# Selection mask of the sparse attention: from a TensorE matmul to a GpSimd add ahead of the logits

## The chip, the cores and the metric

The kernel runs on one core of a Trainium2 chip. The metric is the device time of one execution in microseconds (us), median of three runs. Engines are called by their names in the profile where rows are quoted: PE is TensorE (PEld its weight loads), DVE is VectorE, ACT is ScalarE, POOL is GpSimd, SP issues the DMAs.

## What is computed

Two transformer blocks one after the other on one sequence of 512 tokens of width 1024, in float32. The first has a convolution and retention mixer and an MLP. The second has two kinds of attention with 8 heads of 64 each, a gated merge of the two, and an MLP. The change concerns the second kind of attention, in which every query sees only the keys that an indexer selected:

```python
_, sel = lax.top_k(iscore, topk)               # topk = 128
...
logits = jnp.einsum('bqhd,bqkhd->bhqk', qb, kg) * scale
bias = rel_bias[t5_bucket(dist)]
logits = logits + jnp.transpose(bias, (0, 3, 1, 2))
logits = jnp.where(valid[:, None], logits, -jnp.inf)
p = jax.nn.softmax(logits, axis=-1)
```

The first kind ("forgetting attention") is dense and causal, with a per-key term in place of the bias.

## The kernel before

The kernel is written engine by engine, and each engine runs its instructions in the order written; the order between engines is set by semaphores. There is no planner: what an engine does next is what stands next in its program.

**Precise products.** A float32 product is made of three matmuls on rounded parts: high by high, high by low, low by high. For every 128-column block of weights, SP loads 512 KB into one of four slots of `raw`, ScalarE casts it to `w_hi` (`cast`, L988) and GpSimd makes `w_lo = raw - w_hi` (`lo`, L486). These subtractions are nearly all that GpSimd does. TensorE's `unit` (L526) uses both; it waits for `lo_ready`.

**The attention.** Heads go in pairs: pairs 0 to 3 are the dense attention, pairs 4 to 7 the selected one (`NQ = 4`). A pair has 8 tiles, n = 0 to 7: query block i = n // 2 (128 queries, (i + 1) * 128 keys) of head n % 2. So the tiles of a pair have 128, 128, 256, 256, 384, 384, 512 and 512 keys. "Tile 5.4" below is tile 4 of pair 5. Its way through the engines:

1. `s_step` on TensorE: query times keys into one of two PSUM banks (bank SA for even n, the next for odd n), as two matmuls (L809, L810) and a third that adds the mask through an identity matrix: in pairs 4 to 7 the selection's mask `sel` (L813, bf16, all keys of the tile), in pairs 0 to 3 the causal mask on the last 128 keys (L815). `sel` holds 0 for a selected key and -3e38 for any other. The step waits until the logits of the tile two before it, which used the same bank, are done (`att_logit`).
2. `logits` on VectorE (L1890): adds the table `tab2` (bias by position) to the PSUM bank, scales, writes to the tile's buffer `prob(n)` in SBUF and takes the row's extreme `mneg`. There are four such buffers, so it waits until the transposes of the tile four before are done (`att_t`, `LOOK = 4`).
3. `exps` on ScalarE (L1278), in place, with the row sums.
4. `weights` on VectorE for two tiles at once: a reciprocal (L1896) and two multiplications of `prob` in place (L1899).
5. `t_step` on TensorE: transposes into PSUM (L823); copies out by VectorE (`turned_even`, L1905) and ScalarE (`turned_odd`, `turned_last`); then `pv`, probabilities times values (L836).

**The order of a step.** TensorE's loop goes over p (pair) and n: some steps begin with a `pv`; then come `t_step` of tile p.n, `s_step` of the tile four later, and a piece of a projection: two of the eight k of a `unit`, six matmuls. "Step 4.7" below is this step for p = 4, n = 7. The projections make the queries (slot 0) and keys (slot 1) of pair p + 2, and at the end the first gates of the merge.

VectorE's order (`att`), by n: at even n `weights` of the next two tiles, then `turned_even` (n < 6), then the logits of the tile four later. Besides: at n = 2 `y_lows` (L1909) after the logits, at n = 3 `k_lows` ahead of them (L1925, L1927: low parts of the next pair's keys, for which `s_step` of the next pair's tile 0 waits), at n = 7 `q_lows`, in pairs 0 to 3 rounds of the indexer's selection at n = 1, 4, 5, 6, and in pairs 5 to 7 at n = 2, 4, 5 a piece of the first block's final norm (`final_norm`, L1804, two SBUF inputs).

ScalarE's order, by n of the step: exp of tile n + 4 throughout; `y_evac` and `k_hi` after n = 1; the cast for slot 1 after n = 3; `turned_last` and `q_hi` (two parts) around n = 6; the cast for slot 0 after n = 7.

GpSimd's order in the attention is only `lo` for slot 0 and slot 1 in turn, each as soon as its cast is done. SP loads the weights of a pair, then its table; the table of pair g waits for the logits of pair g - 2, and a slot's load waits for `lo_ready` of that slot.

Of the kernel before, what the change touches and what calls it, by code (L numbers as in the profile page):

```python
# [27 lines left out]
ALU = mybir.AluOpType  # L28
ACT = mybir.ActivationFunctionType

P = 128
T = 512
# [4 lines left out]
NQ = QW // P  # L37
# [17 lines left out]
LOOK = 4  # L55
# [113 lines left out]
def build(nc, tab, x, norm1_g, w_in, conv_w, conv_norm_g, ret_norm_g, w_out, norm2_g, w_up, w_down,  # L169
# [14 lines left out]
    st_att = Stage(st_val, 2 * NQ, 2)  # L184
    st_bra = Stage(st_att, KC, 3, [1, 1, 2, 1])
    bra_order = [(0, 0), (1, 0), (0, 1), (1, 1), (2, 0), (0, 2)]
# [11 lines left out]
    with ctx:  # L198
# [5 lines left out]
        def sem(name):  # L204
            if name not in sems:
                sems[name] = ctx.enter_context(nc.semaphore(name))
            return sems[name]
# [16 lines left out]
        identb, causalb = sb("identb", [P, P], BF16), sb("causalb", [P, P], BF16)  # L224
# [25 lines left out]
        start = ExitStack()  # L250
# [28 lines left out]
        q_up, q_dn = sb("q_up", [P, 4, T], F32R, where=merge), sb("q_dn", [P, 4, T], F32R, where=merge)  # L279
# [5 lines left out]
        k_both = sb("k_both", [P, 4, T], F32R, where=two)  # L285
        tab2 = sb("tab2", [P, 4, T], where=two)
        sel = sb("sel", [P, NT, T], BF16, where=two)
# [25 lines left out]
        def prob(n):  # L313

            return (prob_evens, prob_odds)[n // 2 % 2][:, n % 2, 0:(n // 2 + 1) * P]
# [160 lines left out]
        @block.gpsimd  # L476
        def _(pool):
            for s in range(1, SLOTS):
                pool.sem_inc(lo_ready[s], 1)
            pool.memset(ones[:], 1.0).then_inc(sem("const"), 1)  # L480
            pool.memset(epsc[:], EPS).then_inc(sem("const"), 1)

            def lo(st, s, i):

                pool.wait_ge(hi_ready[s], st.turn(s, i) + 1)
                pool.tensor_tensor(w_lo[:, s, :], raw[:, s, :], w_hi[:, s, :], ALU.subtract  # L486
                                   ).then_inc(lo_ready[s], 1)

            for half in range(2):
                c = slice(half * NQ * P, (half + 1) * NQ * P)  # L490
                pool.wait_ge(hi_ready[0], half + 1)
                pool.tensor_tensor(w_lo[:, 0, c], raw[:, 0, c], w_hi[:, 0, c], ALU.subtract).then_inc(lo_ready[0], 1)
            for s in range(1, SLOTS):
                lo(st_ret, s, 0)
            with pool.Fori(1, NQ) as i:
                for s in range(SLOTS):
                    lo(st_ret, s, i)
            for st in (st_conv, st_out, st_mlp, st_idx, st_val, st_att, st_bra, st_out2, st_mlp2):
                if st is st_bra:
                    for s, m in bra_order:  # L500
                        lo(st_bra, s, m)
                elif st.n == 1:
                    for s in range(st.k):
                        lo(st, s, 0)
                else:
                    with pool.Fori(0, st.n) as i:
                        for s in range(st.k):
                            lo(st, s, i)
# [3 lines left out]
        def _(pe):  # L512
# [287 lines left out]
            def s_step(p, n):  # L800
                i, hh = n // 2, n % 2
                if n == 0:
                    pe.wait_ge(sem("q_ready"), 2 * p + 3)
                    pe.wait_ge(sem("k_ready"), 2 * p + 2)
                wait(pe, sem("att_logit"), 8 * p + n - 1)
                keys = (i + 1) * P
                bank, at = SA + hh, 2 * (p % 2) + hh
                q = slice(i * P, (i + 1) * P)
                pe.matmul(ps[:, bank, 0:keys], q_up[:, at, q], k_both[:, at, 0:keys], start=True, stop=False)  # L809
                pe.matmul(ps[:, bank, 0:keys], q_dn[:, at, q], k_both[:, at, 0:keys], start=False, stop=False)  # L810
                if p >= NQ:
                    pe.wait_ge(sem("sel_ready"), i + 1)
                    last = pe.matmul(ps[:, bank, 0:keys], identb[:], sel[:, i, 0:keys], start=False, stop=True)  # L813
                else:
                    last = pe.matmul(ps[:, bank, keys - P:keys], identb[:], causalb[:], start=False, stop=True)  # L815
                last.then_inc(sem("att_s"), 1)

# [614 lines left out]
        def _(dve):  # L1432
# [446 lines left out]
            def logits(p, n):  # L1879
                keys = (n // 2 + 1) * P  # L1880
                if n == 0:
                    dve.wait_ge(sem("tab_in"), 16 * (p + 1))
                dve.wait_ge(sem("att_s"), 8 * p + n + 1)
                wait(dve, sem("att_t"), 8 * p + n + 1 - LOOK)
                if p < NQ:
                    tab = tab2[:, 2 * (p % 2) + n % 2, 0:keys]
                else:
                    tab = tab2[:, 2 * (p % 2) + n % 2, T - keys:T]

                dve.tensor_tensor_reduce(prob(n), ps[:, SA + n % 2, 0:keys],  # L1890
                                         tab, -(HD ** -0.5), -MASKED, ALU.add, ALU.min,
                                         mneg[:, n:n + 1]).then_inc(sem("att_logit"), 1)
# [141 lines left out]
```

## Time and profile before

| | |
|---|---|
| median of 3 runs (lowest, highest) | 1399.9 us (1398.48, 1400.33) |
| the profiled execution: its time, its span | 1399.89 us, 1398.1 us |
| busy share of the span: PE, DVE, ACT, POOL | 98%, 58%, 37%, 41% |
| the attention of pairs 4 to 7, from the first mask to the last | 780.4 to 859.8 us from the span's start |
| mask matmuls in it (L813) | 32 |

A share of busy time is an average over the whole span; what holds the work up at one place is read from the rows of that place. The end of a matmul in the timeline is modelled, and matmuls overlap, so the cost of one is read from the distances between starts. The profiled execution is within 0.01 us of the median; 1.8 us of it lie outside its span.

### The profile page before, as it was taken

How to read it: one execution, taken by the hardware profiler on the slowest of the kernel's cores; microseconds unless marked ns; L12 is line 12 of the kernel's file. 1: busy time of each engine (PE TensorE's matmuls, PEld its weight loads, DVE VectorE, ACT ScalarE, POOL GpSimd, SP SyncE). 2: the span in 40 equal slices, each digit the busy share in tenths (PEclk: the TensorE clock that was granted, in tenths of full speed). 3: DMA queues.
4: the chain of work that ended last, by engine and by line, in shares of the span. 5: the costliest groups of instructions: out<-in, count | busy, mean ns of one | idle time of the engine just before them, and what ended most of it. 6: DMA issues, size and time to landing. Idle time of an engine off the chain costs nothing.

```text
span 1398.1 us, 18553 instructions
## 1 busy us (share of the span) xinstructions
PE 1369.5 (98%) x6374; PEld 1103.4 (79%) x6374; DVE 808.5 (58%) x1062; ACT 517.7 (37%) x783; POOL 569.4 (41%) x230
## 2 busy tenths in 40 slices
PE   7999999999999999999999999999989999999997
PEld 6777778888888888887777777888868888888886
DVE  4555568584766747886988865343346334252353
ACT  4332224331322314235366664322344223142243
POOL 3433335353562635424322223444425536356341
PEclk9999999999999999989999999999999999999999
DMA  7653234365573754703223232332423323233221
GB/s 205 143 93 95 61 106 156 98 176 157 145 223 108 207 158 131 194 31 109 73 76 91 56 95 77 98 98 81 122 61 113 108 80 113 75 105 109 85 77 60
DMA packets 238993, 155.58 MB, mean 111 GB/s; under 512 B 7860, under 2 KB 229424, under 8 KB 238808
## 3 DMA queue, kind: packets, MB, share of 16 engines
q1 hardware_dynamic: 238472, 153.56, 39.3%
q10 hardware_dynamic: 464, 1.27, 0.3%
q8 instruction: 35, 0.57, 0.2%
q14 instruction: 22, 0.18, 0.0%
HBM read 150.08 MB, written 4.73 MB: 111 GB/s over the span
## 4 chain that ended last, share of the span: by engine, by line
PE 50%; DVE 2%; ACT 1%; issue 0%; POOL 0%; DVEq 0%; ACTq 0%
PE ps L526 40%; PE ps L918 3%; PE ps L836 2%; PE ps L823 2%; PE ps L859 2%; PE ps L809 1%; PE ps L810 1%; DVE work L1871 1%; DVE work L1868 0%; PE ps L813 0%; DVE work L1853 0%; DVE top L1851 0%; POOL w_lo L486 0%; DVE otok L2010 0%; PE ps L815 0%
## 5 line engine op out<-in xcount | busy, mean ns | idle before, releaser
L486 POOL TENSOR_TENSOR w_lo<-raw,w_hi 128x1024 fp32r<-128x1024 f32 x222 | 566.0, 2559 | 796.7 <-ACT w_hi L988 792.1
L526 PE MATMUL ps<-u_hi,w_hi 128*128 128x512 f32 x1016 | 410.5, 404 | 9.9 <-DVE u_lo L1481 3.8
L526 PE MATMUL ps<-u_hi,w_lo 128*128 128x512 f32 x1016 | 398.0, 392 | 0.0
L526 PE MATMUL ps<-u_lo,w_hi 128*128 128x512 f32 x1016 | 397.6, 391 | 0.0
L988 ACT ACTIVATE w_hi<-raw 128x1024 fp32r<-128x1024 f32 x221 | 231.3, 1053 | 233.5 <-PE ps L526 111.6
L526 PEld LDWEIGHTS ps<-u_hi,w_hi 128*128 128x128 f32 x1016 | 192.9, 190 | 52.7 <-issue 8.1
L526 PE MATMUL ps<-y_hi,w_hi 128*128 128x512 f32 x576 | 226.6, 393 | 0.1
L526 PE MATMUL ps<-y_hi,w_lo 128*128 128x512 f32 x576 | 224.2, 389 | 0.0
L526 PE MATMUL ps<-y_lo,w_hi 128*128 128x512 f32 x576 | 224.2, 389 | 0.0
L526 PEld LDWEIGHTS ps<-u_hi,w_lo 128*128 128x128 f32 x1016 | 191.7, 189 | 41.1
L526 PEld LDWEIGHTS ps<-u_lo,w_hi 128*128 128x128 f32 x1016 | 192.3, 189 | 39.0 <-issue 1.9
L1728 DVE TENSOR_TENSOR nt<-nsq 128x512 f32<-128x512 f32 x64 | 82.9, 1296 | 138.1 <-ACT nsq L1184 134.9
L526 PEld LDWEIGHTS ps<-y_hi,w_lo 128*128 128x128 f32 x576 | 108.1, 188 | 22.9
L1750 DVE TENSOR_TENSOR nt<-ps,nrs 128x512 f32<-128x512 f32 x64 | 44.2, 690 | 141.6 <-PE ps L526 138.0
L526 PEld LDWEIGHTS ps<-y_hi,w_hi 128*128 128x128 f32 x576 | 108.2, 188 | 22.4 <-POOL w_lo L486 0.5
L526 PEld LDWEIGHTS ps<-y_lo,w_hi 128*128 128x128 f32 x576 | 108.2, 188 | 21.9 <-issue 0.2
L1184 ACT ACTIVATE nsq<-ps 128x512 f32<-128x512 f32 x64 | 38.0, 594 | 218.5 <-PE ps L526 218.3
L1733 DVE TENSOR_TENSOR y_lo<-nt,y_hi 128x512 f32 x64 | 93.1, 1455 | 13.2 <-DVE nt L1728 6.9
L1701 DVE SCALAR_TENSOR_TENSOR acc<-adaw,vec,acc 128x1536 f32 (+1 forms) x28 | 72.2, 2579 | 4.3 <-DVE y_lo L1733 4.0
L1007 ACT ACTIVATE nsq<-xres 128x512 f32<-128x512 f32 (+1 forms) x32 | 20.1, 628 | 94.2 <-DVE xres L1754 35.4
L1186 ACT ACTIVATE y_hi<-nsq 128x512 f32 x64 | 40.5, 632 | 8.5
L1754 DVE TENSOR_TENSOR xres<-nt,xres 128x512 f32<-128x512 f32 (+1 forms) x32 | 39.9, 1248 | 3.1 <-DVE nt L1750 2.6
(251 smaller groups left out, 1407.0 us busy)
## 6 DMA issues: line engine op xcount, KB each, us to landing
raw<-w_in SPq DMA_DIRECT2D x69, 512.0 KB, 3.8
raw<-w_mlp SPq DMA_DIRECT2D x64, 512.0 KB, 4.0
adaw<-w_ada SPq DMA_DIRECT2D x32, 768.0 KB, 4.5
raw<-w_up SPq DMA_DIRECT2D x32, 512.0 KB, 6.1
raw<-w_down SPq DMA_DIRECT2D x32, 512.0 KB, 6.6
raw<-w_out SPq DMA_DIRECT2D x16, 512.0 KB, 3.9
bias_rows<-fbrow SPq DMA_DIRECT2D x4, 640.0 KB
xtok<-x SPq DMA_DIRECT2D x4, 512.0 KB, 6.0
```

What stands on the lines that cost most here:

```text
L486: pool.tensor_tensor(w_lo[:, s, :], raw[:, s, :], w_hi[:, s, :], ALU.subtract).then_inc(lo_ready[s], 1)
L526: last = pe.matmul(ps[0:cols, bank, :], w[:, s, c], r[:, k, :], start=(k == ks[0] and w is w_hi and r is r_hi), stop=(k == ks[-1] and w is ...
L823: last = pe.transpose(ps[:, TURNS[hh], j * P:(j + 1) * P], prob(n)[:, j * P:(j + 1) * P], ident)
L918: last = pe.matmul(ps[:, b, :], w[:, 2, c], r[:, k, :], start=(k == k0 and w is w_hi and r is y_hi), stop=(k == k0 + NQ - 1 and w is w_lo))
L988: act.activation(w_hi[:, s, :], raw[:, s, :], ACT.Copy).then_inc(hi_ready[s], 1)
L1184: act.activation(nsq[:, s % 2, :], ps[:, s, :], ACT.Relu).then_inc(bank_free[s], 1)
L1186: act.activation(y_hi[:, ds(i * 4 + s, 1), :], nsq[:, s % 2:s % 2 + 1, :], ACT.Square).then_inc(sem("mlp_hi"), 1)
L1701: dve.scalar_tensor_tensor(a, adaw[:, b, :], c, a, ALU.mult, ALU.add).then_inc(sem("acc_done"), 1)
L1728: dve.tensor_tensor(nt[:, s % 2, :], nsq[:, s % 2, :], nsq[:, s % 2, :], ALU.mult).then_inc(sem("mlp_sq"), 1)
L1733: dve.tensor_tensor(y_lo[:, m, :], nt[:, s % 2:s % 2 + 1, :], y_hi[:, m, :], ALU.subtract).then_inc(sem("mlp_h"), 1)
L1750: dve.tensor_tensor(nt[:, 0, :], ps[:, s, :], factor[:], ALU.mult).then_inc(bank_free[s], 1)
L1754: dve.tensor_tensor(xres[:, ds(m, 1), :], nt[:, 0:1, :], xres[:, ds(m, 1), :], ALU.add).then_inc(sem("mlp_x"), 1)
```

## The change

In pairs 4 to 7 the third matmul of `s_step` goes, and with it TensorE's wait for `sel_ready`. In its place GpSimd adds the mask and the position table and puts the sum into `prob(n)`, the buffer that the logits are written to afterwards; the logits take their table from there. GpSimd waits for the table's load (`tab_in`), for the selection and for the buffer to come free; the logits wait for GpSimd (`masks`). GpSimd's program of the attention is written out step by step for this: from step 3.4 on, `masked_table` of the tile four later stands in each step, then at n = 4 the `lo` of slot 1 and at n = 7 the `lo` of slot 0. The first three `lo` of the merge move into this loop, in their old order. Nothing else moves, and no DMA is added or taken away.

```diff
+            def masked_table(p, n):
+                i, tile = n // 2, 8 * p + n
+                keys = (i + 1) * P
+                pool.wait_ge(sem("tab_in"), 16 * (p + 1))
+                pool.wait_ge(sem("sel_ready"), i + 1)
+                pool.wait_ge(sem("att_t"), tile + 1 - LOOK)
+                pool.tensor_tensor(prob(n), tab2[:, 2 * (p % 2) + n % 2, T - keys:T], sel[:, i, 0:keys], ALU.add
+                                   ).then_inc(sem("masks"), 1)
...
-                if st is st_bra:
-                    for s, m in bra_order:
+                if st is st_att:
+                    with pool.Fori(0, NQ + 1) as i:
+                        for s in range(st.k):
+                            lo(st, s, i)
+                    lo(st, 0, NQ + 1)
+                    for p in range(NQ - 1, 2 * NQ):
+                        for n in range(8):
+                            tile = 8 * p + n + LOOK
+                            if 8 * NQ <= tile < 16 * NQ:
+                                masked_table(tile // 8, tile % 8)
+                            if n == 4 and p + 2 < 2 * NQ:
+                                lo(st, 1, p + 2)
+                            if n == 7 and p + 3 < 2 * NQ:
+                                lo(st, 0, p + 3)
+                            if (n == 7 and p + 3 == 2 * NQ) or (n == 4 and p + 2 == 2 * NQ):
+                                lo(st_bra, int(n == 4), 0)
+                            if n == 7 and p + 2 == 2 * NQ:
+                                lo(st_bra, 0, 1)
+                elif st is st_bra:
+                    for s, m in bra_order[3:]:
                         lo(st_bra, s, m)
...
                 pe.matmul(ps[:, bank, 0:keys], q_up[:, at, q], k_both[:, at, 0:keys], start=True, stop=False)
-                pe.matmul(ps[:, bank, 0:keys], q_dn[:, at, q], k_both[:, at, 0:keys], start=False, stop=False)
-                if p >= NQ:
-                    pe.wait_ge(sem("sel_ready"), i + 1)
-                    last = pe.matmul(ps[:, bank, 0:keys], identb[:], sel[:, i, 0:keys], start=False, stop=True)
-                else:
+                last = pe.matmul(ps[:, bank, 0:keys], q_dn[:, at, q], k_both[:, at, 0:keys], start=False, stop=(p >= NQ))
+                if p < NQ:
                     last = pe.matmul(ps[:, bank, keys - P:keys], identb[:], causalb[:], start=False, stop=True)
                 last.then_inc(sem("att_s"), 1)
...
                 else:
-                    tab = tab2[:, 2 * (p % 2) + n % 2, T - keys:T]
+                    tab = prob(n)
+                    dve.wait_ge(sem("masks"), 3 + 8 * (p - NQ) + n + 1)
```

## Rows read from the trace of the kernel before

**Rows 1.** Windows, one pair each: us, busy time by engine, clock, DMA
```profile
759.67:779.80 20.13, 20.13 (x134) 15.14 (x132) 16.92 (x48) 12.96 (x30) 4.91 (x2) 1.00 0.29 79
779.80:800.27 20.47, 20.47 (x134) 15.39 (x132) 17.80 (x46) 12.74 (x30) 4.84 (x2) 1.00 0.28 78
```
**Rows 2.** Chain of waits between 780 and 862 us, shares by line
```profile
by line: PE ps L526 54.6%; PE ps L823 13.9%; PE ps L836 13.6%; PE ps L810 6.2%; PE ps L809 6.1%; PE ps L813 5.9%
```
**Rows 3.** Timeline of TensorE around two masks: start, us, engine, line, operation
```profile
780.37 0.23 PE L813 MATMUL ps<-sel,identb 128*128 128x128 bf16 x1
...
780.72 0.40 PE L526 MATMUL ps<-u_lo,w_hi 128*128 128x512 f32 x1
...
795.87 0.39 PE L813 MATMUL ps<-sel,identb 128*128 128x512 bf16 x1
...
796.33 0.39 PE L526 MATMUL ps<-u_lo,w_hi 128*128 128x512 f32 x1
796.56 0.40 PE L526 MATMUL ps<-u_hi,w_lo 128*128 128x512 f32 x1
```
**Rows 4.** Timeline of GpSimd in the attention
```profile
803.13 2.39 POOL L486 TENSOR_TENSOR w_lo<-raw,w_hi 128x1024 fp32r<-128x1024 f32 x1 [9.26 <-ACT w_hi L988]
811.43 2.38 POOL L486 TENSOR_TENSOR w_lo<-raw,w_hi 128x1024 fp32r<-128x1024 f32 x1 [5.92 <-ACT w_hi L988]
823.98 2.39 POOL L486 TENSOR_TENSOR w_lo<-raw,w_hi 128x1024 fp32r<-128x1024 f32 x1 [10.17 <-ACT w_hi L988]
833.25 2.52 POOL L486 TENSOR_TENSOR w_lo<-raw,w_hi 128x1024 fp32r<-128x1024 f32 x1 [6.87 <-ACT w_hi L988]
...
862.78 5.20 POOL L486 TENSOR_TENSOR w_lo<-raw,w_hi 128x1024 fp32r<-128x1024 f32 x2 [7.94 <-ACT w_hi L988]
```
**Rows 5.** Instructions of line L492: duration ns min/median/max, first and last start
```profile
L492 POOL TENSOR_TENSOR w_lo<-raw,w_hi x2: 1275/1508/1742, 9.1 to 10.4; 128x512 fp32r<-128x512 f32 x2
```
**Rows 6.** Timeline of VectorE in the attention
```profile
803.86 0.29 DVE L1890 CUSTOM_DVE_ANT_0 prob_evens<-ps,tab 128x128 f32<-128x128 f32 x1
...
811.54 2.68 DVE L1899 TENSOR_SCALAR prob_odds<-prob_odds,rinv 128x256 f32<-128x256 f32 x2 [0.22 <-DVE rinv L1896]
...
820.45 0.69 DVE L1927 TENSOR_TENSOR k_both<-ps,k_both 64x512 fp32r<-64x512 f32 x1
...
824.66 2.27 DVE L1804 SCALAR_TENSOR_TENSOR xres<-xres,vec,rfin 128x512 f32<-128x512 f32 x1
826.85 0.28 DVE L1890 CUSTOM_DVE_ANT_0 prob_evens<-ps,tab 128x128 f32<-128x128 f32 x1
...
832.90 0.62 DVE L1899 TENSOR_SCALAR prob_odds<-prob_odds,rinv 128x256 f32<-128x256 f32 x2
...
835.12 0.56 DVE L1890 CUSTOM_DVE_ANT_0 prob_evens<-ps,tab 128x384 f32<-128x384 f32 x1 [0.81 <-PE ps L813]
...
840.37 0.69 DVE L1927 TENSOR_TENSOR k_both<-ps,k_both 64x512 fp32r<-64x512 f32 x1
...
863.25 2.47 DVE L1804 SCALAR_TENSOR_TENSOR xres<-xres,vec,rfin 128x512 f32<-128x512 f32 x1
```
**Rows 7.** Timeline of ScalarE: exp of tile 6.1, cast of slot 0
```profile
827.17 0.40 ACT L1278 ACTIVATE prob_evens<-prob_evens,mneg 128x128 f32<-128x128 f32 x1 [1.52 <-DVE mneg L1890]
...
832.12 1.05 ACT L988 ACTIVATE w_hi<-raw 128x1024 fp32r<-128x1024 f32 x1
```
**Rows 8.** Timeline of TensorE: score steps of tiles 5.6, 6.0, 6.6, 7.0
```profile
815.78 0.48 PE L809 MATMUL ps<-k_both,q_up 128*128 128x512 f32 x1
...
821.24 0.30 PE L809 MATMUL ps<-k_both,q_up 128*128 128x128 f32 x1
...
836.44 0.48 PE L809 MATMUL ps<-k_both,q_up 128*128 128x512 f32 x1
...
841.70 0.31 PE L809 MATMUL ps<-k_both,q_up 128*128 128x128 f32 x1
```
**Rows 9.** DMA issues of weights in one pair: start, us until issued
```profile
801.74 4.21 SPq L330 DMA_DIRECT2D raw<-w_in  x2
```

## Prediction

> **What bounds the kernel now.** I read first the busy time by engine, then the windows of single pairs, then the chain of waits through the last four pairs, then the timelines of each engine in two of them. The windows show TensorE busy for the whole of each pair, at full clock: 20.13 us in a dense pair, 20.47 us in a masked one [rows 1]. In the chain from 780 to 862 us every step is a TensorE line, the mask's included with 5.9% of 82 us, 4.8 us [rows 2]. So TensorE sets the time here, and what is taken from it is won as long as the others keep up. Whether they do is the question: the others are not full, but they are chained in a fixed order, and two of their links are already close to TensorE. Tile 6.0's score step starts at 821.24, 0.10 us after VectorE's low parts of the keys that it reads (820.45 + 0.69 = 821.14): no slack [rows 6, 8].
>
> **What the removed matmul gives.** At 512 keys the mask starts at 795.87 and the second projection matmul behind it at 796.33; one projection matmul takes 0.23 us from start to start (796.33 to 796.56) [rows 3]. The mask therefore costs 796.33 - 795.87 - 0.23 = 0.23 us; at 128 keys 780.72 - 780.37 - 0.23 = 0.12. The same reading for 256 and 384 keys lies between them, 0.13 and 0.18. Two tiles of each size: 1.32 us a pair, **5.3 us** in four pairs (the chain's 4.8 us agrees). Bounds: if the two small sizes gave nothing, because the projection's first weight load was hidden under them, 3.3 us; no more than 5.3. I take 5.3. TensorE's wait for the selection had ended long before and gives nothing.
>
> **What the added instruction costs.** Per pair eight two-input adds on GpSimd. None with bf16 is in the trace; the nearest rows are the same operation on float32: 1024 columns in 2.39 us [rows 4], 512 in 1.275 us, the shorter of two [rows 5]. So 0.17 us and 2.2 ns a column: 0.45, 0.72, 1.00 and 1.27 us for 128 to 512 keys, 6.9 us a pair. With the two subtractions GpSimd is busy 11.7 of 20 us. Load isn't the trouble, order is. Lower bound by rows: no fixed part, 2.33 ns a column (384 keys: 0.90). Upper: 0.25 us and 2.5 ns, from the 2.52 us row with a margin for the mixed types.
>
> **What the new wait is queued behind.** GpSimd's queue is now masks, a `lo`, masks, a `lo`. A `lo` starts only when ScalarE has cast, and the mask behind it waits for cast and `lo` both. I follow it through the tiles of pair 5, from the rows between 800 and 821 us.
>
> - The `lo` of slot 1 runs 803.13 to 805.52 [rows 4]. Mask 5.1 comes behind it: 805.97. Its logits start at 806.0, not at 803.86 [rows 6]: 2.1 us late.
> - From that logit (826.85 in the next pair) its exp starts 0.32 us later, and from exp to the cast of slot 0 ScalarE works through in 4.95 us (827.17 to 832.12) [rows 6, 7]. So the cast starts at 811.3, and the `lo`, 1.13 behind as at 833.25, runs 812.4 to 814.8, a microsecond later than before [rows 4].
> - Mask 5.4 is next: 815.8. Logits 5.4, 0.55 us: ready at 816.45.
> - The score step of tile 5.6 needs them (same bank). It stood at 815.78 [rows 8] and would now be due at 814.9, since six masks ahead of it (0.12, 0.12, 0.13, 0.13, 0.18, 0.18) are gone. TensorE waits **1.5 us**.
> - Mask 5.5 ends at 816.8 and its logits start there. From these logits to the end of the low parts of the keys VectorE's and ScalarE's chain takes 841.06 - 835.12 = 5.94 us [rows 6], so 822.8, and tile 6.0's score step can start at 822.9. TensorE is there at 816.45 + (841.70 - 836.44) - 2 x 0.23 = 821.2 [rows 8]. It waits **1.7 us**.
>
> In pair 6 the same way, with one thing more: the final norm's instruction with two SBUF inputs stands still while GpSimd works (824.66 to 826.93, over the `lo` that ends at 826.37) [rows 4, 6] and then goes ahead of GpSimd's next. Mask 6.1 ends at 827.4, its logits are 0.6 late, the `lo` of slot 0 runs 833.85 to 836.25, mask 6.4 to 837.25, logits 6.4 to 837.9; due 836.44 - 0.86 = 835.6. Waits: **2.3 us**, then again **1.7**. In pair 4 VectorE's multiplications are caught by the `lo` of slot 0 as they are now, mask 4.4 follows them: **1.9 us**; and then **0.9**, for there is no final norm yet. In pair 7 ScalarE has no more query projection to round and gains about as much as the mask costs: **0.7 us**, and no second wait. Sum of the waits 1.9 + 1.5 + 2.3 + 0.7 + 0.9 + 1.7 + 1.7 = **10.7 us**.
>
> Against 5.3 us won this is +5.4 us. Some smaller ones (tile n.2 behind its turned copy, the key projection's piece behind the `lo` of slot 1, which had 0.4 us to spare) are of 0.2 us each; against them, a TensorE that has waited leaves the others ahead. I put these at zero. 1399.89 + 5.4 = **1405.3 us**; the profiled execution is the median, so no correction.
>
> What is moved otherwise costs nothing. SP's loads wait for `lo_ready`, at most 2 us later, and of the two loads issued from 801.74 [rows 9] the first one used is the one whose `lo` runs at 823.98, its cast a microsecond ahead of it [rows 4]; a pair's table is issued just before them. The three `lo` of the merge stay in order.
>
> **The port between VectorE and GpSimd.** The multiplications of `prob` take 0.62 us for two where GpSimd is idle and 2.68 us where a `lo` has begun 0.11 us before them: they end 0.4 us after it ends [rows 4, 6]. GpSimd's second instruction in a row of two is in turn 0.42 us late (5.20 against 2 x 2.39) where a final norm waited (863.25, 2.47 us) [rows 4, 6]: the one that waits goes first. This is what I used. The Trainium skill (SBUF — State Buffer, "Who interferes with whom") says that the pair of ports is an exclusive lock, that the second to issue blocks fully, and that VectorE instructions with two SBUF inputs or in a two-port mode are concerned. By that rule each of the eight adds a pair is one more time in which VectorE can be held, and the trace agrees in every row named. The same page's summary advises to put on the contended port what is off the critical path; the mask was on TensorE's path and now hangs on that of the logits.
>
> **Rivals.**
>
> - *Hidden mask (faster).* The adds are ready before the logits want them, and 5.3 us stay: 1394.6; or, with the low parts of the keys as the limit (no slack now, above), some 1.5 us: 1398. For it: GpSimd idles 8 us a pair. Against: it must have mask n.4 done by 814.3 in pair 5 for the score step at 814.9, and `lo` alone ends at 814.8. It decides if the cast of slot 0 comes 2 us earlier than I reckon, which it can only if the mask n.1 isn't held by the `lo` of slot 1.
> - *Draw.* Adds at the lower bound take about 1.6 us from the waits, the small masks' slack on ScalarE as much again: 1402 and below.
> - *Much slower.* GpSimd keeps the ports through a row of adds and VectorE's waiting multiplication comes last. With `lo`, mask n.4 and n.5 back to back (4.4 us) the turned copy, which TensorE's next transposes wait for, then the logits come 1 to 1.5 us later in each pair: +10 to 11. Or the add costs the upper bound: 0.2 us more on each of three adds in the chain and two chains a pair: +4, so 1409. Both: 1415. The row at 863.25 speaks against the first.
> - *TensorE wins less* (3.3 us): 1407, part of my own case.
>
> **How the numbers follow.** My case, 1402.8 to 1408: 0.53. Much slower, above 1408: 0.22. Draw, within 2.8 us (0.2%, about what can be told from no change here): 0.14. Faster: 0.11. Slower in all 0.75. The range leaves out the faster case but for its upper edge, and what lies above both bounds: 1398 to 1415.
>
> **What would show it.** Right: L813 gone, the windows of pairs 4 to 7 longer than 20.47 us, about 21 to 23, with TensorE idle ahead of L809 of tiles n.6 and of the next pair's tile 0, released by VectorE, and GpSimd's adds in a row behind each `lo`. The adds take 0.45 to 1.27 us. The rest of the span keeps its length. Wrong: masked pairs of about 19.2 us, or adds well under 0.4 us; or logits of tile n.4 that don't start right at the end of an add. The weakest step is the chain from the logits n.1 to the cast of slot 0, each link of which is taken from another pair than it is used for.

## The result, and the profile after

The changed kernel takes 1407.06 us, the median of 5 runs (1405.14 to 1409.85), against 1400.17 us of the kernel before beside it (5 runs, 1398.48 to 1400.33). The ratio is 1.0049, with a 95% interval of 1.0038 to 1.0059: slower by 6.9 us, where 1405.3 us was predicted. The profiled execution took 1407.06 us with a span of 1404.9 us, 6.8 us longer than the span before.

The busy times by engine, from the page of the kernel after:

```profile
PE 1368.6 (97%) x6342; PEld 1102.8 (78%) x6342; DVE 807.9 (58%) x1062; ACT 517.6 (37%) x783; POOL 594.5 (42%) x262
```

The windows of the kernel after, first the four masked pairs (from the first transposes of step n.4 to those of the next pair; columns as in [rows 1]), then the whole stretch from the first transposes of step 3.4 to the first product of the merge's gates:

```profile
780.04:801.20 21.16, 19.79 (x126) 14.98 (x124) 17.13 (x45) 12.70 (x30) 11.10 (x10) 1.00 0.28 76
801.20:823.08 21.88, 19.99 (x126) 15.14 (x124) 11.52 (x37) 12.78 (x31) 11.09 (x10) 1.00 0.27 73
823.08:846.10 23.02, 20.04 (x127) 15.13 (x124) 15.00 (x40) 12.82 (x31) 11.53 (x10) 1.00 0.34 92
846.10:868.00 21.90, 20.26 (x129) 15.25 (x126) 13.74 (x39) 10.62 (x27) 11.39 (x10) 1.00 0.27 73
...
780.04:881.21 101.17, 93.03 (x584) 70.33 (x583) 62.62 (x165) 55.51 (x126) 52.66 (x43) 1.00 0.29 79
```

The same stretch of the kernel before:

```profile
779.80:874.65 94.85, 94.85 (x617) 71.49 (x615) 63.89 (x165) 55.65 (x126) 26.85 (x11) 1.00 0.31 84
```

It grew from 94.85 to 101.17 us: 6.3 of the 6.8 us by which the span grew are here (the bounds of the last three pairs are up to 0.1 us off the starts of their transposes, 823.16, 846.20 and 867.90). Before, TensorE was busy in all of it; now it is busy 93.03 us and idle 8.1 us. The granted clock is 1.00 in both. The masked pair of 20.47 us in [rows 1] became one of 21.2 to 23.0 us.

What it waits for, in the waits of TensorE in the kernel after, 779 to 880 us (total, times, longest):

```profile
PE ps L837 <- DVE mneg L1916: 4.3, 4, 1.8
PE ps L837 <- issue: 2.7, 3, 1.1
PE ps L848 <- DVE probt_even L1931: 0.7, 1, 0.7
PE ps L554 <- POOL w_lo L486: 0.3, 1, 0.3
```

L837 is the first matmul of the score step (L809 before), L1916 the logits. The timeline of TensorE after shows which tiles they are: the transposes and the score step of tile 4.6, the score step of tile 5.0, then those of 5.6, 6.0, 6.6 and 7.0, the four of [rows 8], and last that of tile 7.6:

```profile
795.51 0.41 PE L848 MATMUL ps<-small,prob_odds 128*128 128x128 f32 x2 [0.67 <-DVE probt_even L1931]
796.61 0.50 PE L837 MATMUL ps<-k_both,q_up 128*128 128x512 f32 x1 [0.69 <-DVE mneg L1916]
...
802.23 0.30 PE L837 MATMUL ps<-k_both,q_up 128*128 128x128 f32 x1 [0.47 <-issue]
...
818.56 0.50 PE L837 MATMUL ps<-k_both,q_up 128*128 128x512 f32 x1 [1.35 <-DVE mneg L1916]
...
824.84 0.30 PE L837 MATMUL ps<-k_both,q_up 128*128 128x128 f32 x1 [1.14 <-issue]
...
841.60 0.50 PE L837 MATMUL ps<-k_both,q_up 128*128 128x512 f32 x1 [1.78 <-DVE mneg L1916]
...
847.88 0.30 PE L837 MATMUL ps<-k_both,q_up 128*128 128x128 f32 x1 [1.13 <-issue]
...
863.30 0.50 PE L837 MATMUL ps<-k_both,q_up 128*128 128x512 f32 x1 [0.45 <-DVE mneg L1916]
```

The waits called "issue" have no releaser in the trace. The timeline of VectorE (below) gives one: its last low part of the keys runs from 824.05 to 824.74, and the score step that reads it starts at 824.84.

The number in brackets is not the whole of a wait. It is counted from the modelled end of the matmul before, and the ends of matmuls in a row overlap the next starts by 0.1 to 0.2 us, an overlap that a wait loses. From start to start a wait is longer. Tile 5.6 before (its score step is in [rows 8]), then after:

```profile
815.65 0.38 PE L823 MATMUL ps<-small,prob_odds 128*128 128x128 f32 x2
```

```profile
816.83 0.38 PE L848 MATMUL ps<-small,prob_odds 128*128 128x128 f32 x2
```

Before, the score step starts 0.13 us after these transposes (815.78), now 1.73 us after them (818.56). The wait has cost 1.60 us where the bracket says 1.35.

One turn of the loop, in the kernel after. GpSimd from 805 us:

```profile
805.00 2.40 POOL L486 TENSOR_TENSOR w_lo<-raw,w_hi 128x1024 fp32r<-128x1024 f32 x1 [2.65 <-ACT w_hi L1013]
807.36 0.43 POOL L496 TENSOR_TENSOR prob_evens<-tab,sel 128x128 f32<-128x128 f32 x1
...
814.37 2.53 POOL L486 TENSOR_TENSOR w_lo<-raw,w_hi 128x1024 fp32r<-128x1024 f32 x1 [3.02 <-ACT w_hi L1013]
816.85 1.78 POOL L496 TENSOR_TENSOR prob_evens<-tab,sel 128x384 f32<-128x384 f32 x2
```

VectorE in the same time:

```profile
807.96 0.29 DVE L1916 CUSTOM_DVE_ANT_0 prob_evens<-ps,prob_evens 128x128 f32<-128x128 f32 x1 [2.20 <-POOL prob_evens L496]
...
817.93 0.56 DVE L1916 CUSTOM_DVE_ANT_0 prob_evens<-ps,prob_evens 128x384 f32<-128x384 f32 x1 [2.96 <-POOL prob_evens L496]
...
822.56 0.74 DVE L1829 SCALAR_TENSOR_TENSOR xres<-xres,vec,rfin 128x512 f32<-128x512 f32 x1
...
824.05 0.69 DVE L1953 TENSOR_TENSOR k_both<-ps,k_both 64x512 fp32r<-64x512 f32 x1
```

And ScalarE, the exp of tile 5.1 and the cast of slot 0:

```profile
808.29 0.41 ACT L1303 ACTIVATE prob_evens<-prob_evens,mneg 128x128 f32<-128x128 f32 x1 [1.63 <-DVE mneg L1916]
...
813.24 1.05 ACT L1013 ACTIVATE w_hi<-raw 128x1024 fp32r<-128x1024 f32 x1
```

Read across the three fences. Mask 5.1 stands behind the `lo` of slot 1 and starts 807.36, as that ends. Its logits start at 807.96, having waited 2.20 us. Exp follows at 808.29, the cast of slot 0 at 813.24, its `lo` at 814.37, mask 5.4 at 816.85, logits 5.4 at 817.93 (after a wait of 2.96 us) and the score step of tile 5.6 at 818.56, 1.35 us late. TensorE's wait is named as one for VectorE, but VectorE was itself waiting for GpSimd, and GpSimd for ScalarE.

All of the adds together, in the groups of GpSimd by form, kernel after, 779 to 881 us (busy us, mean ns, idle before and its releaser):

```profile
L496 POOL TENSOR_TENSOR prob_odds<-tab,sel 128x512 f32<-128x512 f32 x8 | 9.4, 1171 | 5.2 <-PE ps L848 5.2
L496 POOL TENSOR_TENSOR prob_evens<-tab,sel 128x384 f32<-128x384 f32 x8 | 7.2, 918 | 0.0
L496 POOL TENSOR_TENSOR prob_odds<-tab,sel 128x256 f32<-128x256 f32 x8 | 5.4, 675 | 8.2 <-PE ps L848 8.2
L496 POOL TENSOR_TENSOR prob_evens<-tab,sel 128x128 f32<-128x128 f32 x8 | 4.3, 541 | 11.6 <-PE ps L848 11.6
```

GpSimd waited 25.0 us for transposes that had to free the buffers (6.7 of them ahead of the very first add); an idle time of an engine off the chain costs nothing by itself. The masks of 384 keys never waited at all: they stood behind a `lo` each time. The chain's head line also says that the bound is shared now; in [rows 2] it was TensorE alone. The chain of waits after, 780 to 869 us:

```profile
by line: PE ps L554 32.5%; issue 15.7%; PE ps L848 10.2%; PE ps L861 8.1%; PE ps L837 4.9%; PE ps L838 3.6%; POOL prob_evens L496 3.1%; POOL w_lo L486 3.0%; DVE prob_evens L1916 2.8%; DVE prob_odds L1925 2.8%; DVE prob_odds L1916 2.2%; DVE 
```

### The profile page after: what moved, and what is told of

The parts are those of the page before. It is cut to its first block, busy times and chain, and to the rows that moved or that the text cites. A ratio compares the mean times of both kernels' runs of the same rounds, so it can differ in the third digit from the quotient of the medians.

```text
span 1404.9 us, 18549 instructions
## 1 busy us (share of the span) xinstructions
PE 1368.6 (97%) x6342; PEld 1102.8 (78%) x6342; DVE 807.9 (58%) x1062; ACT 517.6 (37%) x783; POOL 594.5 (42%) x262
## 3 DMA queue, kind: packets, MB, share of 16 engines
q10 hardware_dynamic: 464, 1.27, 0.3%
## 4 chain that ended last, share of the span: by engine, by line
PE 48%; DVE 3%; issue 1%; ACT 1%; POOL 1%; DVEq 0%; POOLq 0%; ACTq 0%
PE ps L554 39%; PE ps L943 3%; PE ps L884 2%; PE ps L848 1%; PE ps L861 1%; PE ps L837 1%; PE ps L838 1%; POOL w_lo L486 1%; DVE work L1896 1%; DVE work L1878 0%; DVE top L1876 0%; DVE work L1893 0%; DVE prob_odds L1925 0%; DVE prob_evens L1916 0%; POOL prob_evens L496 0%
```

## Experiments

Each experiment is an edit of the changed kernel but for one, which edits the kernel before. "Stretch" is the time from the first transposes of step 3.4 to the first product of the gates, 94.85 us before and 101.17 after, read from one profiled execution each. Medians are compared with the kernel before on the same chip: 1400.35 us beside the first four, 1400.67 beside the next four, 1400.51 beside the last four.

### No mask at all

```diff
-                            if 8 * NQ <= tile < 16 * NQ:
-                                masked_table(tile // 8, tile % 8)
...
-                    tab = prob(n)
-                    dve.wait_ge(sem("masks"), 3 + 8 * (p - NQ) + n + 1)
+                    tab = tab2[:, 2 * (p % 2) + n % 2, T - keys:T]
```

> As the changed kernel, but the selection's mask is left out altogether: no matmul for it, no add on GpSimd, no wait; the logits take the position table as before. Tells what the removed matmuls give if nothing is put in their place. Theory (the other engines' fixed order is nearly as long as TensorE's): part of the 5.3 us is taken back by TensorE waiting for the low parts of the next pair's keys at tile 0, so 3.3 us less than the kernel before, about 1396.9, with waits of 0.3 to 0.5 us at tile 0 of pairs 6 and 7. Rival (all of the removed work is won): 5.3 us less, 1394.9, and no such waits. Second rival (the projection's first weight load was hidden under the small masks): 3.3 us less too, but then without waits and with a step at 128 keys that is not 0.12 us shorter.

1399.30 us; ratio 0.9990 (0.9981 to 0.9999). Its window of the stretch:

```profile
779.53:871.98 92.45, 91.23 (x584) 70.08 (x583) 63.62 (x165) 55.65 (x126) 26.84 (x11) 1.00 0.31 86
```

Its timelines of VectorE in pair 4 and of TensorE at tile 5.0:

```profile
791.02 2.74 DVE L1922 TENSOR_SCALAR prob_odds<-prob_odds,rinv 128x256 f32<-128x256 f32 x2
...
800.13 0.30 PE L835 MATMUL ps<-k_both,q_up 128*128 128x128 f32 x1 [0.47 <-issue]
```

The stretch is only 2.4 us shorter than before, the median 1.1 us. Even a mask that costs nothing anywhere wins less than half of the matmuls' price. TensorE now waits for the low parts of the keys at tiles 5.0 and 6.0 (0.5 and 0.7 us; the theory had named 6.0 and 7.0), and VectorE's multiplications are still held by a `lo`; the kernel with the `lo` in halves, below, bears on those. This is less than my own theory gave (3.3 us), and far from the rival's 5.3.

### The matmul kept and the add too

```diff
+                if p >= NQ:
+                    pe.wait_ge(sem("zeros"), 1)
+                    pe.wait_ge(sem("sel_ready"), i + 1)
+                    last = pe.matmul(ps[:, bank, 0:keys], zerob[:], sel[:, i, 0:keys], start=False, stop=True)
```

> As the changed kernel, but the third matmul stays beside the add, at the same size, with a weight matrix of zeros (it adds nothing; GpSimd clears that matrix once before the attention). So TensorE has all of its old work and the new wait. Theory (the pace of pairs 4 to 7 is now set by the loop GpSimd, VectorE, ScalarE, and TensorE stands waiting): the 5.3 us of matmuls fit into the waits, the time stays within 1.5 us of the changed kernel, 1406 to 1408.5. Rival (the waits come on top of TensorE's work): 5.3 us more, 1412.

1406.29 us; ratio 1.0040 (1.0026 to 1.0054). Its window and its waits of TensorE:

```profile
781.99:883.12 101.13, 96.65 (x616) 71.61 (x615) 62.59 (x165) 55.52 (x126) 52.62 (x43) 1.00 0.28 79
```

```profile
PE ps L840 <- DVE mneg L1923: 2.9, 3, 1.3
PE ps L840 <- issue: 1.5, 2, 0.7
```

TensorE does the 32 matmuls again, and the stretch lasts 101.13 us against 101.17: the removed work now fits in the waits. This is what the theory said, and the median is inside its range. So the time is set by the loop through GpSimd, not by what is left on TensorE.

### Adds of the same size that nobody reads

```diff
-                pool.tensor_tensor(prob(n), tab2[:, 2 * (p % 2) + n % 2, T - keys:T], sel[:, i, 0:keys], ALU.add
+                pool.tensor_tensor(nrs[:, 0:keys], rfin[:, T - keys:T], sel[:, i, 0:keys], ALU.add
...
-                    tab = prob(n)
-                    dve.wait_ge(sem("masks"), 3 + 8 * (p - NQ) + n + 1)
+                    tab = tab2[:, 2 * (p % 2) + n % 2, T - keys:T]
```

> As the changed kernel, with the same eight adds per pair on GpSimd, of the same sizes and in the same order among the subtractions, but from another table into a buffer that nobody reads; the logits take the position table and don't wait for GpSimd. The mask is thereby left out. Each add also waits for the add before it. Keeps GpSimd's load and its hold on the shared port and takes away only that the logits wait. Theory (the loss comes from the logits waiting in GpSimd's order): most of it goes, 1399 to 1401, about 3 us more than with no mask at all; the difference to that one is the port and the later subtractions. Rival (the port: VectorE's multiplications and norms held by the adds): the time stays above 1404.

1402.15 us; ratio 1.0017 (1.0008 to 1.0026). By the medians, each against its own kernel before, the unread adds cost 1.8 + 1.05 = 2.9 us over no mask, and making the logits wait for them costs 6.9 - 1.8 = 5.1 us more. Two things blur this. The unread adds are not quite the change's: each also waits for the one before, so those in a row start 0.17 us apart. And in the stretch, where the split is 4.5 and 4.2 us (92.45, 96.96, 101.17), this profile ran its last pair at a granted clock of 0.92, so its 4.5 is an upper figure. The three pairs at full clock take 60.27 us with no mask, 61.43 with the unread adds and 66.16 with the change: 1.2 us for the adds and 4.7 for the waiting. So the waiting is the larger part by either reading, as the theory said, and the rival's "above 1404" did not come. The timeline of GpSimd in this kernel, and below it that of VectorE, show how an unread add can cost:

```profile
811.02 2.37 POOL L486 TENSOR_TENSOR w_lo<-raw,w_hi 128x1024 fp32r<-128x1024 f32 x1 [1.53 <-ACT w_hi L1014]
813.34 0.97 POOL L497 TENSOR_TENSOR nrs<-rfin,sel 128x384 f32<-128x384 f32 x1
```

```profile
811.15 3.31 DVE L1925 TENSOR_SCALAR prob_odds<-prob_odds,rinv 128x256 f32<-128x256 f32 x2 [0.23 <-DVE rinv L1922]
```

Two multiplications, 0.62 us where GpSimd is idle, take 3.31 us: they are held over the `lo` and over the add behind it, to 814.46. In the changed kernel itself no multiplication was held that long: the longest pair of them took 2.75 us, the other three 0.61 or 0.62.

### The `lo` of slot 0 behind two masks instead of ahead of them

```diff
-                            if n == 7 and p + 3 < 2 * NQ:
-                                lo(st, 0, p + 3)
...
+                            if n == 1 and p >= NQ:
+                                if p + 2 < 2 * NQ:
+                                    lo(st, 0, p + 2)
+                                else:
+                                    lo(st_bra, 0, p + 2 - 2 * NQ)
```

> As the changed kernel, but the subtraction for slot 0 stands behind the masks n.4 and n.5 (in the step n = 1 of the next pair) and not ahead of them. Theory (mask n.4 is late because it stands behind a subtraction that waits for ScalarE's cast): the waits at tile n.6 (0.7 to 1.8 us a pair) go, those at tile 0 stay for the final norm's and the masks' order, 3.2 us less than the changed kernel, 1404. Rival (the adds' duration itself or the port is what costs): less than 1 us changes.

1404.80 us; ratio 1.0036 (1.0022 to 1.0050). Its waits of TensorE, 779 to 880 us:

```profile
PE ps L555 <- POOL w_lo L486: 4.2, 4, 1.1
```

The waits of the score steps n.6 are gone, and the projection behind them stands for its `w_lo` instead, 1.05 us in each of four pairs. The wait moved and became smaller: the stretch is 98.07 us, 3.1 less than the change's, and by the medians, each against its own kernel before, the gain is 2.4 us (4.5 against 6.9). The theory had 3.2 us, with the n.6 waits gone and nothing in their place; the rival, under 1 us, is out.

### The final norm's first piece a step later

```diff
-                    if p > NQ and n in (2, 4, 5):
-                        m = 3 * (p - NQ - 1) + (2, 4, 5).index(n)
+                    if p > NQ and n in (3, 4, 5):
+                        m = 3 * (p - NQ - 1) + (3, 4, 5).index(n)
```

> As the changed kernel, but of the three pieces of the final norm in pairs 5 to 7 the one in step n = 2, ahead of the low parts of the keys, is done in step n = 3 behind them. Theory (tile 0 of the next pair waits for the low parts of the keys, and the norm's 0.7 us stand in that chain): the waits at tile 0 of pairs 6 and 7 (1.1 us each) shrink by about 0.7 us each, 1.5 to 2 us less than the changed kernel, about 1405. Rival (those waits come from the late masks n.5 and n.6 alone): no change.

1405.87 us; ratio 1.0039 (1.0025 to 1.0052). Its waits of TensorE:

```profile
PE ps L837 <- DVE mneg L1916: 4.2, 4, 1.8
PE ps L837 <- issue: 1.4, 3, 0.5
```

The waits at tile 0 fall from 2.7 to 1.4 us, those at n.6 stay (4.3 and 4.2); the stretch is 99.33 us, 1.8 less. The piece of the norm, 0.74 us ahead of the low parts of the keys, was part of the second wait. The medians, each against its own kernel before, agree with 1.7 us (5.2 against 6.9), but their intervals overlap; the profile carries this reading.

### No mask, norm late

The two edits above together.

> The kernel without any mask (no matmul, no add; the mask is left out) with the norm's piece moved behind the low parts of the keys as in the run before. The most that the removal of the matmuls can give once that piece is out of the way. Theory: the window from pair 5 to 6 falls by 0.7 us, the others stay; 1398.5, still not the 1395 that 5.3 us would give, because the subtraction for slot 0 and VectorE's chain behind it hold pairs 4 and 5. Rival (only the norm stood in the way): 1395 to 1396.

1397.75 us; ratio 0.9978 (0.9968 to 0.9987); stretch 91.67 us. Its window of the last masked pair has no wait of TensorE in it:

```profile
839.87:859.12 19.25, 19.25 (x126) 15.01 (x125) 13.13 (x39) 11.56 (x29) 4.77 (x2) 1.00 0.31 83
```

Against the 20.47 us of a masked pair before ([rows 1]; pair 7 before, 841.40 to 861.87, takes the same), this is what the matmuls of a pair are worth, 1.22 us: 4.9 us in four. Of that a free mask wins 3.2 us (94.85 - 91.67), the most that a placing of the mask can give with the rest of this kernel as it is. The norm's move is worth 0.8 us of it (92.45 to 91.67), as the theory said; the rival's 1395 to 1396 did not come.

### Masks by matmul at three tiles, by GpSimd at five

```diff
+                added = p >= NQ and n not in (1, 4, 5)
...
+                if p >= NQ and not added:
+                    pe.wait_ge(sem("sel_ready"), i + 1)
+                    last = pe.matmul(ps[:, bank, 0:keys], identb[:], sel[:, i, 0:keys], start=False, stop=True)
```

GpSimd leaves out the same tiles, and the norm is late.

> Only tiles 0, 2, 3, 6, 7 of each pair get their mask from GpSimd; tiles 1, 4, 5, whose add would stand directly behind a subtraction, keep the matmul and the table. The norm's piece stands in step n = 3. Theory (the adds hurt by where they stand, not by what they take): no waits at tile n.6, TensorE saves 0.85 us a pair, 3.4 in all, less what tile 0 takes back: 1398 to 1399, 8 us under the changed kernel and a little under the one before. Rival (GpSimd's load and the port hurt wherever the adds stand): 1402 or more.

1399.39 us; ratio 0.9992 (0.9983 to 1.0001); stretch 93.51 us. TensorE's waits are two of 0.4 us. The late norm alone has 99.33 us with all eight masks on GpSimd: taking 1, 4 and 5 out of GpSimd's queue wins 5.8 us, though TensorE has three matmuls a pair again, and it is a draw with the kernel before. This changes two things at once, where the adds stand and how many there are (five for eight). No run took three others out, so the place alone is not shown here; the run with tiles 4, 5 and 6 below says more of it.

### The `lo` of slot 0 behind one mask, norm late

The edit of the `lo` above with `n == 0` for `n == 1`.

> As the changed kernel with all masks on GpSimd, but the subtraction for slot 0 stands behind mask n.4 only (in step n = 0), and the norm's piece in step n = 3. With the subtraction behind two masks the projection waited 1.05 us a pair for it. Theory: one mask less ahead of it takes these 1.05 us away, mask n.4 is early, mask n.5 late by up to 1 us; 1401 to 1402. Rival (the wait only moves again, to the projection or to tile n.7): 1404 as with two.

1404.37 us; ratio 1.0027 (1.0018 to 1.0036); stretch 97.84 us. Its waits of TensorE, 779 to 880 us:

```profile
PE ps L862 <- DVE y_lo L1936: 1.7, 1, 1.7
PE ps L838 <- issue: 1.4, 3, 0.5
PE ps L849 <- DVE probt_even L1932: 1.2, 2, 0.7
```

They are in other places again: a `pv` behind the low part of the output, the transposes behind the turned copy. This is the rival's figure (1404), not the theory's 1401 to 1402. The granted clock was 0.98 over this stretch. Neither of the two places tried for this `lo` among the masks is free.

### An extra add of 128 columns ahead of each mask

```diff
+                wait(pool, sem("extra"), tile - 8 * NQ)
+                pool.tensor_tensor(nrs[:, 0:P], sel[:, 0, 0:P], sel[:, 0, 0:P], ALU.add).then_inc(sem("extra"), 1)
```

> As the changed kernel, with one more add of 128 columns on GpSimd ahead of each mask, into a buffer that nobody reads (it waits for the one before it). Each mask comes 0.35 to 0.45 us later. Theory (GpSimd's masks stand in the loop that sets the pace, about two to three of them a pair): 1 us or more a pair, 5 to 8 us over the changed kernel, 1412 to 1415, with TensorE's added waits at tiles n.6 and n + 1.0. Rival (GpSimd has room, it idles half of these pairs): within 2 us of the changed kernel.

1412.62 us; ratio 1.0085 (1.0069 to 1.0101), 5.2 us more over its own kernel before than the change has (12.1 against 6.9). Its waits of TensorE, 781 to 888 us:

```profile
PE ps L839 <- DVE mneg L1918: 6.8, 4, 2.5
```

The waits at n.6 grow from 4.3 to 6.8 us. GpSimd's queue sets the time by its order, since it is still busy only 65 of 105.5 us of this stretch. The profile can't split the 5.2 us by pair: pairs 5 and 6 ran at a granted clock of 0.93 (0.97 over the whole stretch), and of the two at full clock pair 4 is 1.1 us longer than in the change (22.23 against 21.16), pair 7 no longer (21.74 against 21.70). The lower edge of the 5 to 8 us forecast is met by the medians, and the two intervals don't touch.

### The kernel before with the norm late

The norm's edit alone, on the kernel before.

> The kernel before with one edit: the norm's piece of step n = 2 in step n = 3. For reading the mixed kernel. Theory (TensorE is busy throughout in the kernel before, but for 0.2 us at tile 0 of pair 6): 0 to 0.4 us less, nothing that can be measured. Rival (the norm's place is what the mixed kernel won by): 1 us less or more.

1400.62 us; ratio 1.0003 (0.9994 to 1.0012); stretch 94.66 us. The norm's place is worth nothing while TensorE sets the time.

### Matmul masks at tiles 4, 5 and 6

The mixed kernel again, with other tiles; then the same with the `lo` of the last pairs in two halves, so that an instruction of VectorE can come in between. The norm is late in both:

```diff
+                    c = slice(0, NQ * P)
+                    pool.tensor_tensor(w_lo[:, s, c], raw[:, s, c], w_hi[:, s, c], ALU.subtract
+                                       ).then_inc(sem("half_lo"), 1)
+                    c = slice(NQ * P, KC * P)
+                    pool.wait_ge(sem("half_lo"), halves)
+                    pool.tensor_tensor(w_lo[:, s, c], raw[:, s, c], w_hi[:, s, c], ALU.subtract
+                                       ).then_inc(lo_ready[s], 1)
```

> Masks of tiles 4, 5, 6 by the matmul, of 0, 1, 2, 3, 7 by GpSimd, the norm's piece in step n = 3. Against the mixed kernel before, mask n.6 leaves the chain to the low parts of the keys and mask n.1 comes back behind the subtraction for slot 1. Theory: TensorE saves 0.74 us a pair; the attention is as long as in the mixed kernel with tiles 1, 4, 5 on TensorE, within 0.7 us; about 1399. Rival (a mask behind the subtraction for slot 1 delays the cast of slot 0 by 2 us as in the prediction's chain, and that is what costs): 1 us longer or more.

> As the run before, but GpSimd's subtractions of the last pairs are done in two halves of 512 columns (each half waits for the one before). VectorE's multiplications for tiles n.2 and n.3, which stand 2.4 us behind a whole subtraction, can go in between. Theory (this hold is the other half of the chain that keeps TensorE from using its saved work in pairs 4 and 5): 0.5 to 1 us less than the run before in the attention. Rival (halves cost two instructions' start and come later than the whole): 0.5 us more.

Whole `lo`: 1399.54 us, ratio 0.9995 (0.9986 to 1.0004), stretch 93.58. In halves: 1399.32 us, ratio 0.9990 (0.9981 to 0.9999). The window of the second:

```profile
779.39:872.36 92.97, 92.69 (x593) 70.25 (x596) 58.94 (x165) 55.73 (x126) 42.37 (x39) 1.00 0.32 86
```

TensorE is busy in all but 0.3 us. The halves shorten the stretch by 0.6 us, all of it in pair 4, where the held multiplications take 1.64 us instead of 2.74; pair 5's were not held in either. The medians, 0.2 us apart, don't show it. Of the kernels that compute the whole, this has the lowest median, about 8 us under the change, but only 1.2 us under the kernel before; that is at the edge of what can be told.

With whole `lo` mask n.1 stands behind the `lo` of slot 1 again, and the `lo` of slot 0 starts late again in pair 5, 12.9 us after the pair's first transposes where the kernel before had 11.2. Yet the stretch is as short as with tiles 1, 4 and 5 out (93.58 against 93.51), so the rival, 1 us longer or more, is out: in this kernel a late cast costs nearly nothing, since no mask of tiles n.4 and n.5 waits behind it. It takes both, a late cast and a mask behind its `lo`, to close the loop.

## Why the prediction was right

**What sets the time: right.** TensorE was full before and now stands for a loop GpSimd, VectorE, ScalarE, GpSimd. The kernel with both masks (stretch 101.13 us against 101.17) and the extra add (+5.2 us) show it from both sides.

**The removed matmul: 5.3 us predicted, 4.9 measured.** The clean pair of the kernel without a mask gives 1.22 us, not 1.32. The chain's share had said 4.8.

**The adds: 0.45, 0.72, 1.00 and 1.27 us predicted; 0.43, 0.68, 0.92 and 1.17 measured** (the 128 keys by the row at 807.36, since holds stretch their mean to 0.54; the others by their mean or their row). The upper bound for the mixed types wasn't needed.

**The waits.** The prediction worked them out as the start of a score step less the start at which it would be due, so they are measured here from start to start too, each matmul laid beside the same one before.

| wait at tile | 4.6 | 5.0 | 5.6 | 6.0 | 6.6 | 7.0 | 7.6 | sum |
|---|---|---|---|---|---|---|---|---|
| predicted, us | 1.9 | 0.9 | 1.5 | 1.7 | 2.3 | 1.7 | 0.7 | 10.7 |
| measured, us | 1.8 | 0.7 | 1.6 | 1.2 | 2.0 | 1.4 | 0.7 | 9.4 |

The first is 0.84 at the transposes and 0.96 at the score step right behind them. All seven stand where they were predicted. The four at n.6 come to 6.1 us for 6.4, the three at tile 0 to 3.3 for 4.3; at tile 6.0 the whole wait is 1.4, but 0.2 of it the kernel before had already (821.24 is 0.50 us behind its transposes at 820.74, the usual distance is 0.31), which the prediction didn't take off.

In pair 5 every link can be laid beside the prediction, counted from the transposes of step 4.4 (800.27 before, 801.20 after): logits 5.1 at +6.8 us (predicted +5.7), cast of slot 0 at +12.0 (+11.0), logits 5.4 at +16.7 (+15.6). The distance from exp to cast came out as 4.95 us, exactly as taken. The whole chain is 1.0 to 1.1 us later than predicted, from its start: the `lo` of slot 1 began at +3.8 instead of +2.9. The score step of tile 5.6 became due later by as much, 816.83 + 0.13 = 816.96, or +15.8 and not +14.6. The prediction took neither shift into account, and they cancel: so the 1.5 us is right by a little luck.

**The small ones: zero predicted, 1.8 us measured,** by what remains: the stretch grew by 6.3 us although 4.9 were taken from it, so 11.2 us were lost, 9.4 of them at the seven. The largest, 0.5 us from start to start, is in this row of TensorE after, the key projection behind the `lo` of slot 1, named in the prediction and then left out:

```profile
872.98 0.50 PE L554 MATMUL ps<-u_hi,w_hi 128*128 128x512 f32 x1 [0.25 <-POOL w_lo L486]
```

Seven more are of 0.1 us each, at the first matmul of a `pv` or of a projection; what delays those I can't say.

So the stretch is 9.4 + 1.8 - 4.9 = 6.3 us longer where the prediction had 10.7 - 5.3 = 5.4. The waits were put 1.3 us too high, the gain 0.4 too high and the small ones 1.8 too low; in part these cancel. The medians add 0.6 us that no row of the stretch explains. The forecast was 1.5 us short of the 6.9 measured.

**The rivals.** The hidden mask fell, and the kernels without a mask show more: even then only 2.4 us are won, 3.2 with the norm moved. The rival's 5.3 us could not be had by any mask, and its lower figure of some 1.5 us was the nearer. The much slower case did not come: in the change no multiplication was held over a mask, and a waiting norm went ahead of the mask, as the row at 863.25 of [rows 6] had said. GpSimd's and VectorE's row in pair 6 after:

```profile
829.96 0.88 POOL L496 TENSOR_TENSOR prob_evens<-tab,sel 128x128 f32<-128x128 f32 x1
```

```profile
828.29 2.27 DVE L1829 SCALAR_TENSOR_TENSOR xres<-xres,vec,rfin 128x512 f32<-128x512 f32 x1
```

The norm, 0.74 us when free, ends at 830.56, after the `lo` (830.01), and the mask takes 0.88 us instead of 0.43. The draw was reached only with three of eight masks back on TensorE.

**The port.** The unread adds cost 2.9 us by the medians with nobody waiting for their data, so about a third of the 7.9 us between no mask and the change is not a wait for the mask; in the three pairs at full clock it is 1.2 of 5.9 us, a fifth. The Trainium skill (SBUF — State Buffer, "Who interferes with whom") says that the shared port pair is an exclusive lock and that issue order decides who blocks. The two multiplications of 3.31 us agree: the first was issued 0.13 us after the `lo`, the second 0.12 us after the add (813.46 against 813.34), and each was held until that one was over. How the 2.9 us divide between held instructions and subtractions that start later behind the adds, I can't say: no run here separates them.

## What to carry to other kernels

Before work is moved from the full engine to an idle one, read the order of the idle one's queue, not its busy share: an item behind an instruction that waits for a third engine inherits that wait, and if that third engine waits for the item's reader, the three form a loop that can be slower than the engine relieved. Price the move first with the work simply left out: here the best possible gain was 2.4 to 3.2 us of 4.9, which none of the placings tried with eight adds a pair could keep. Compare a predicted wait with a measured one in the same measure: from start to start, since the idle time in brackets leaves out the overlap of the matmuls (1.35 for 1.60 us at tile 5.6). And don't put many small waits at zero against a few large ones.

## What the runs showed of the hardware

- **VectorE and GpSimd take turns.** In the kernel with unread adds, where a `lo` had an add queued behind it, VectorE's two multiplications were held over both, 3.31 us for 0.62. The timeline of VectorE in narrow windows (around 813.1 and around 814.5 us) shows the two one by one:

```profile
811.15 2.38 DVE L1925 TENSOR_SCALAR prob_odds<-prob_odds,rinv 128x256 f32<-128x256 f32 x1 [0.23 <-DVE rinv L1922]
```

```profile
813.46 1.00 DVE L1925 TENSOR_SCALAR prob_odds<-prob_odds,rinv 128x256 f32<-128x256 f32 x1
```

The first ends at 813.53, 0.14 us after the `lo` (813.39), and the add took 0.97 us where another of its size beside it took 0.92. The second ends at 814.46, 0.15 us after the add (814.31). So each engine's waiting instruction went before the other's next one. The norm of 828.29 above, between `lo` and mask, is the same.
- **Logits are not held.** Those of tile 5.4 (one input in PSUM, one in SBUF) took 0.56 us from 817.93 while the next mask ran on GpSimd. The same shape before took 0.55 us at 814.46, where GpSimd was idle, and 0.56 at 835.12 [rows 6], under the `lo` of 833.25.
- **A bf16 input costs nothing extra on GpSimd's add, as far as the nearest rows tell:** 1.17 us for 512 columns with one bf16 input, against 1.275 us for the shorter float32 subtraction of [rows 5] and 1.27 for the shortest of 16 in the kernel with halves. Those write fp32r; no run has the same add on two float32 inputs.
